# A mixture-of-experts pass that norms and stores its own tokens: gather, sum, norm and scatter moved from the kernel's end into each pass

## The chip, the cores and the metric

The kernel runs on one core of a Trainium2 chip. Its time is the device time of one execution in microseconds. The core has a matrix engine (TensorE, PE in the profile, with PEld for its weight loads), a vector engine (VectorE, DVE), a scalar engine (ScalarE, ACT), GpSimd (POOL), and SyncE (SP), which here only issues DMAs. Each engine runs its own instruction list in order and waits on semaphores for the others.

## The reference

One transformer layer on 512 tokens of width 1024, all in float32. First `proj = x @ w_in`, and three branches from it (an RWKV-7 scan over 8 heads, a gated spatial unit, a causal depthwise convolution), merged by sigmoid gates, then `x1 = layer_norm(ALPHA * x + merged @ w_out)`. What the change touches is the second half:

```
scores = sigmoid(x1 @ router_w)                    # 32 experts in 4 groups of 8
group  = the group whose two best scores sum highest
expert = the two best experts of that group, gate = their scores, normalised
moe    = sum over the two: gate * ((silu(x1 @ w_gate[e]) * (x1 @ w_up[e])) @ w_down[e])
out    = layer_norm(ALPHA * x1 + moe) * ln2_g + ln2_b
```

A token's two experts lie in one group; call the one with the lower index its lower expert, the other its upper expert.

## The kernel before

The stages follow each other on PE: projections and branches (to 469 us), the merge and `w_out` (to 585 us), the router and the tables of passes (to about 617 us), then the passes of the experts, and the last norm.

A pass (line 1456, `one_pass` of PE) takes up to 64 tokens of one expert. An expert with more than 64 tokens has more passes; here there are 33 for 32 experts, and the sixth expert has two. A token's row of 1024 values is laid over two partitions as two halves of 512, so 64 tokens fill 128 partitions (slots 0 to 63 hold the first halves, 64 to 127 the second). The order of a pass:

- POOL gathers the tokens' rows of `x1` from DRAM into `xe` by an indirect DMA (`gather`, L531), one pass ahead. An index out of bounds moves nothing, so empty slots cost no bytes.
- PE transposes `xe` (L1453) for the next pass; DVE copies it out as `xeT` (L1117).
- PE makes gate and up products (L1464): k = 0 to 7, two column halves, 16 products into each half of bank 0.
- ACT takes the silu (L718), DVE multiplies (L1110), PE transposes `h_e` (L1473), DVE copies (L1113), PE makes the down products (L1484) into bank 1.
- ACT scales the result by the gate into `y_e` (L722), and POOL scatters it to `y_dram` (L545), where a token has one row for its lower and one for its upper expert.

The weights of an expert are 6 chunks of 1 MB. Four sets of chunks are in SBUF. PE raises `s_used` as it is done with a chunk, and SP, which waits for that, issues the load of the same chunk for the expert four further on (`reload`, L450). SP's and POOL's DMAs go through different queues.

After the last passes SP loads `x1` back, the gains of the last norm (L457, L458), the lower rows (L463, as soon as all experts that can be lower are stored) and, after the last scatter, the upper rows in four parts (L467). DVE adds, takes mean and variance over 1024 values and norms each of the four parts of 128 tokens (L1131 to L1147), ACT takes the roots (L740), and SP stores each part (L470). Nothing is planned by a cost model: each engine's list is written out by hand, and semaphores alone set the order.

## Time and profile before

| | us |
|---|---|
| median of 3 runs | 1125.63 (1125.48 to 1126.07) |
| the profiled execution's own time | 1125.88 |
| its span, first to last instruction | 1124.2 |
| PE busy in the span | 982.6 (87%) |
| DVE, ACT, POOL busy | 359.7, 166.8, 123.9 |
| HBM read and written | 256.97 MB, 12.85 MB |
| mean granted TensorE clock | 0.965 of full speed |

The profile is one execution. Busy time counts an engine's instructions without waits. The slices cut the span into 40 equal parts. The chain of waits follows back from the last instruction to what released each step; "SPq" in it is SP issuing DMAs, "DMA a<-b" is a transfer in flight. In a timeline, the bracket says how long the engine was idle before the instruction and what ended that. PEld loads the stationary operand and overlaps PE. A window's row gives each engine's busy time and instruction count, then the granted clock, the DMA engines' busy share and GB/s.

### The profile page before, as it was taken

Reading aid. Unit: us, or ns where it says so; the run is one execution under the profiler, and the core shown is the slowest. Engines: PE = TensorE matmul, PEld = TensorE weight load, DVE = VectorE, ACT = ScalarE, POOL = GpSimd, SP = SyncE. Lnnn points to the kernel's source line nnn. Section 1 sums busy time; section 2 is a strip of 40 time slices with the busy share of each in tenths; the row PEclk is TensorE's granted clock in tenths of the full one; section 3 lists DMA queues with packets and bytes.
Section 4 is the critical chain, followed back from the end, with each engine's and each line's share of the span. In section 5 each row is a group of like instructions: output and inputs, shape, how many; then the busy total and the mean of one; then the engine's idle time right before and its main releaser. Section 6 shows DMA issues by size and latency. Waiting matters only on the chain.

```text
span 1124.2 us, 15343 instructions
## 1 busy us (share of the span) xinstructions
PE 982.6 (87%) x5932; PEld 457.0 (41%) x5933; DVE 359.7 (32%) x674; ACT 166.8 (15%) x304; POOL 123.9 (11%) x192
## 2 busy tenths in 40 slices
PE   7999999999999999999993688888888888887840
PEld 3644475466456457444453233333333333322210
DVE  0695643553463373422445000110000000000018
ACT  1123322312222222200001000000010000000010
POOL 1000010010010010033000111111111111111100
PEclk9999999999999999999995799999999999999985
DMA  8232201211220210573537799999999999999982
GB/s 254 61 92 58 74 22 38 76 39 39 56 58 21 66 48 10 213 295 151 219 115 322 270 420 419 396 419 421 419 419 418 419 421 419 420 420 421 420 316 117
DMA packets 90430, 261.35 MB, mean 232 GB/s; under 512 B 11192, under 2 KB 56248, under 8 KB 65552
## 3 DMA queue, kind: packets, MB, share of 16 engines
q1 hardware_dynamic: 83936, 249.46, 57.4%
q0 software_dynamic: 5648, 9.07, 2.2%
q10 hardware_dynamic: 800, 2.15, 0.5%
q8 instruction: 36, 0.59, 0.2%
q14 instruction: 10, 0.08, 0.0%
HBM read 256.97 MB, written 12.85 MB: 240 GB/s over the span
## 4 chain that ended last, share of the span: by engine, by line
PE 63%; SPq 14%; DVE 10%; DMA 8%; issue 4%; ACT 2%; DVEq 0%; ACTq 0%; POOLq 0%; PEldq 0%
SPq L450 13%; PE proj L1219 11%; PE bank L1464 10%; PE proj L1178 10%; PE bank L1484 6%; PE proj L1399 5%; PE bank L1309 5%; PE bank L1387 5%; DMA xT_sb<-w_gu 3%; DMA arena<-w_gu 2%; DMA gates<-y_rows 2%; PE proj L1186 1%; PE proj L1197 1%; DVE arena L867 1%; DVE arena L1117 1%
## 5 line engine op out<-in xcount | busy, mean ns | idle before, releaser
L1219 PE MATMUL proj<-xT_sb,ring 128*128 128x512 f32 x384 | 182.1, 607 | 0.0
L1110 DVE TENSOR_TENSOR const<-pass_sb,bank 128x256 f32<-128x256 f32 x33 | 13.9, 422 | 408.4 <-ACT pass_sb L718 408.4
L1464 PE MATMUL bank<-arena 128*64 128x512 f32 x544 | 122.2, 596 | 16.2 <-PE bank L1484 11.3
L1178 PE MATMUL proj<-xT_sb,ring 128*128 128x512 f32 (+1 forms) x272 | 119.1, 594 | 0.0
L1219 PEld LDWEIGHTS proj<-xT_sb,ring 128*128 128x128 f32 x384 | 68.2, 189 | 68.3 <-issue 64.8
L1464 PEld LDWEIGHTS bank<-arena 128*64 128x64 f32 x544 | 43.0, 137 | 95.2 <-issue 82.7
L1178 PEld LDWEIGHTS proj<-xT_sb,ring 128*128 128x128 f32 (+1 forms) x272 | 50.8, 188 | 64.6 <-issue 64.5
L1464 PE MATMUL bank<-gates,arena 128*64 128x512 f32 x256 | 59.7, 617 | 8.2 <-PE bank L1484 4.7
L1309 PEld LDWEIGHTS bank<-arena 64*64 64x64 f32 x1536 | 52.8, 134 | 18.2 <-ACT arena L676 9.1
L1309 PE MATMUL bank<-arena 64*64 64x64 f32 (+1 forms) x1536 | 56.5, 228 | 0.0
L1387 PE MATMUL bank<-branches,arena 128*128 128x512 f32 x128 | 55.4, 593 | 0.9 <-DVE branches L961 0.9
L1484 PE MATMUL bank<-arena,const 128*64 128x512 f32 x208 | 48.4, 600 | 8.8 <-DVE const L1113 8.8
L1399 PE MATMUL proj<-arena 128*128 128x512 f32 x128 | 55.4, 592 | 0.0
L545 POOL DMA_INDIRECT y_rows<-const,raw x33 | 33.7, 1020 | 147.7 <-ACT const L722 147.7
L718 ACT ACTIVATE pass_sb<-bank 128x256 f32<-128x256 f32 x33 | 12.7, 384 | 249.2 <-PE bank L1464 249.2
L722 ACT ACTIVATE const<-bank,raw 128x512 f32<-128x512 f32 x33 | 22.7, 687 | 178.7 <-PE bank L1484 178.7
L774 DVE SCALAR_TENSOR_TENSOR arena<-arena,par_sb 128x512 f32<-128x512 f32 x60 | 39.8, 742 | 0.0
L531 POOL DMA_INDIRECT pass_sb<-x_rows,raw x34 | 35.8, 1052 | 26.9 <-POOL raw L528 26.1
L528 POOL COPY raw<-raw 128x1 int32 (+1 forms) x34 | 6.2, 183 | 295.0 <-PE bank L1453 206.9
L1464 PEld LDWEIGHTS bank<-gates,arena 128*64 128x64 f32 x256 | 18.4, 141 | 49.1 <-issue 43.2
L1387 PEld LDWEIGHTS bank<-branches,arena 128*128 128x128 f32 x128 | 24.2, 190 | 31.9 <-issue 30.1
L676 ACT ACTIVATE arena<-bank 128x256 f32<-128x256 f32 (+1 forms) x64 | 27.5, 436 | 64.6 <-PE bank L1309 59.6
(259 smaller groups left out, 1011.1 us busy)
## 6 DMA issues: line engine op xcount, KB each, us to landing
arena<-w_gu SPq DMA_DIRECT2D x64, 1024.0 KB, 24.6
gates<-w_gu SPq DMA_DIRECT2D x32, 1024.0 KB, 21.9
arena<-w_down SPq DMA_DIRECT2D x24, 1024.0 KB, 24.7
ring<-w_in SPq DMA_DIRECT2D x42, 512.0 KB, 3.9
gates<-w_down SPq DMA_DIRECT2D x16, 1024.0 KB, 23.5
branches<-w_down SPq DMA_DIRECT2D x16, 1024.0 KB, 25.9
xT_sb<-w_gu SPq DMA_DIRECT2D x16, 1024.0 KB, 26.4
ring<-w_gu SPq DMA_DIRECT2D x16, 1024.0 KB, 25.8
```

What stands on the lines that cost most here:

```text
L450: sp.dma_start(w_chunk[b][c], src.rearrange("a p n -> (a p) n")).then_inc(s_w[b][c], 16)
L531: pool.indirect_dma_start(xe, None, x1_dram, bass.IndirectOffsetOnAxis(ap=idx_now[:, 0:1], axis=0), bounds_check=last_half_row, oob_is_err ...
L545: pool.indirect_dma_start(y_dram, bass.IndirectOffsetOnAxis(ap=row_now[:, 0:1], axis=0), y_e, None, bounds_check=last_row, oob_is_err=Fals ...
L676: ins = act.activation(d, bank[:, 3 * g + b, 0:TT * n].rearrange("p (j n) -> p j n", j=TT), ACT.Copy)
L774: ins = dve.scalar_tensor_tensor(conv_acc[:, i, :], src, w, conv_acc[:, i, :], MUL, ADD)
L1178: ins = pe.matmul(proj[0:w, b, :], ring[:, slot, k, 0:w], xT_sb[:, k, :], start=(k == 0), stop=(k == KT - 1))
L1219: ins = pe.matmul(proj[:, gate_at["bank"], :], ring[:, gate_at["slot"], k, :], xT_sb[:, k, :], start=(k == 0), stop=(k == KT - 1))
L1309: ins = pe.matmul(bank[t, 3 * g + b, j * n:j * n + n], lhsT[t, j, :], rhs[t, j, :], start=True, stop=True)
L1387: ins = pe.matmul(bank[:, 3 * (m % 2) + n, :], wo_sb[:, k0 + k, m * P:(m + 1) * P], src[:, k, :], start=(k == 0), stop=(k == nk - 1))
L1399: ins = pe.matmul(proj[:, n % 2, :], merged[:, k, c * P:(c + 1) * P], wout_sb[:, k, T * i:T * i + T], start=(k == 0), stop=(k == KT - 1))
L1464: ins = pe.matmul(bank[SLOTS * h:SLOTS * h + SLOTS, 0, :], xeT[:, k % 4, SLOTS * (k // 4):SLOTS * (k // 4) + SLOTS], gu[k // 2][:, k % 2, ...
L1484: ins = pe.matmul(bank[SLOTS * h:SLOTS * h + SLOTS, 1, :], hT[:, f % 2, SLOTS * (f // 2):SLOTS * (f // 2) + SLOTS], wd[f // 2][:, f % 2, h ...
```

## The change

In each pass, the tokens for which its expert is the upper one are finished. Their lower rows are already in `y_dram`, because experts run in order of index.

- `y_dram` now has one row per token, for the lower expert alone. It is zeroed early by eight DMAs on POOL. POOL scatters `y_e` there with `low_tab`, whose index is out of bounds for upper tokens (`scatter_lower`).
- POOL gathers, with `up_tab`, the lower rows of a pass's upper tokens into `y_low` (`lower_rows`), after the last pass's lower scatter has landed.
- ACT copies the token rows times ALPHA from `xe` into PSUM, by turns bank 5 and bank 4 (`keep_rows`); the next token gather waits for that too.
- DVE (`finish`) adds `y_low`, then `y_e`, into `x2`, and takes mean and variance over each half row (512 values). The two halves of a token sit on different partitions: PE adds them by a product with `ident_twice` (`pair_stats`), at k = 4 of the next pass's gate and up products. Then DVE and ACT make the deviation, and DVE scales twice, with the gains now in the two banks of `proj`.
- POOL scatters `x2` to the output with `up_tab` (`scatter_out`).
- `h_silu` and `h_e` now share one place, and `hT` too; the extra pass's ACT work waits for one bank more.
- SP's reloads at the end, the last norm and the four stores are gone. SP loads the gains (4 DMAs of 64 partitions x 2 KB) when the tables are ready.

POOL's order in a pass p is now: the token gather of p+2, the lower scatter of p, the output scatter of p, the lower rows of p+1. DVE's is: products of p, then `finish` of p.

```diff
+        x_now, ln2_g, ln2_b = (bank[:, 5, :], bank[:, 4, :]), proj[:, 0, :], proj[:, 1, :]
+        pair = bank[:, 3, FE // 2:FE // 2 + 2]
...
+            sp.wait_ge(s_more, 1)
+            for i, dst in ((0, y_e), (1, x2)):
+                for h in range(2):
+                    at = 2 * SGU + 2 * D + D * i + T * h
+                    sp.dma_start(dst[SLOTS * h:SLOTS * h + SLOTS, :],
+                                 rows[:, at:at + T].partition_broadcast(SLOTS).rearrange("p a d -> p (a d)")).then_inc(s_lnback, 16)
...
-            sp.wait_ge(s_used, (N_EXP - 3) * NCH + 1)
...
-            sp.dma_start(y_lower, y_rows[0]).then_inc(s_lower, 16)
-            more = sp.value_load(more_i[0:1, 0:1], min_val=0, max_val=MORE)
-            sp.wait_ge(s_yst, more * 16 + 16 * N_EXP)
-            for c in range(TT):
-                sp.dma_start(y_upper[:, c, :], y_rows[1, :, c, :]).then_inc(s_upper[c], 16)
-            for c in range(TT):
-                sp.wait_ge(s_x2[c], 1)
-                sp.dma_start(out[c * P:(c + 1) * P, :], x1_back[:, c, :]).then_inc(s_st, 16)
-            sp.wait_ge(s_st, 16 * TT)
...
+            for n in range(T // SLOTS):
+                pool.dma_start(y_dram.rearrange("(n s h) d -> n s (h d)", s=SLOTS, h=2)[n], zeros).then_inc(s_y0, 16)
...
+            def lower_rows(p, first=False):
+                pool.tensor_copy(up_now[:, 0:1], up_tab[:, bass.ds(p, 1)]).then_inc(s_up, 1)
+                pool.wait_ge(s_up, p + 1)
+                if not first:
+                    pool.wait_ge(s_yst, p * 16)
+                pool.sem_inc(s_begun, 1)
+                pool.indirect_dma_start(y_low, None, y_dram, bass.IndirectOffsetOnAxis(ap=up_now[:, 0:1], axis=0),
+                                        bounds_check=last_half_row, oob_is_err=False).then_inc(s_ylow, 16)
+            def scatter_lower(p):
+                pool.tensor_copy(low_now[:, 0:1], low_tab[:, bass.ds(p, 1)]).then_inc(s_low, 1)
+                pool.wait_ge(s_low, p + 1)
                 pool.wait_ge(s_ye, p + 2)
                 pool.sem_inc(s_begun, 1)
-                pool.indirect_dma_start(y_dram, bass.IndirectOffsetOnAxis(ap=row_now[:, 0:1], axis=0), y_e, None,
-                                        bounds_check=last_row, oob_is_err=False).then_inc(s_yst, 16)
-            def one_pass(p):
-                next_tokens(p + 2)
-                pool.wait_ge(s_yst, p * 16 + 16)
-                scatter(p + 1)
+                pool.indirect_dma_start(y_dram, bass.IndirectOffsetOnAxis(ap=low_now[:, 0:1], axis=0), y_e, None,
+                                        bounds_check=last_half_row, oob_is_err=False).then_inc(s_yst, 16)
+            def scatter_out(p, first=False):
+                if not first:
+                    pool.wait_ge(s_ost, p * 16)
+                pool.tensor_copy(out_now[:, 0:1], up_tab[:, bass.ds(p, 1)]).then_inc(s_outidx, 1)
+                pool.wait_ge(s_outidx, p + 1)
+                pool.wait_ge(s_x2, p + 1)
+                pool.sem_inc(s_begun, 1)
+                pool.indirect_dma_start(out_dram, bass.IndirectOffsetOnAxis(ap=out_now[:, 0:1], axis=0), x2, None,
+                                        bounds_check=last_half_row, oob_is_err=False).then_inc(s_ost, 16)
+            def one_pass(p, first=False):
+                next_tokens(p + 1)
+                scatter_lower(p)
+                scatter_out(p, first)
+                pool.wait_ge(s_ylow, p * 16 + 16)
+                lower_rows(p + 1)
...
+            scatter_out(more + (N_EXP - 1))
...
+            def keep_rows(p, n):
+                act.wait_ge(s_xe, p * 16 + 16)
+                act.activation(x_now[n], xe, ACT.Copy, scale=ALPHA).then_inc(s_xnow, 1)
+            def one_pass(p, n, first=False):
                 act.activation(warm[:, 1:2], warm[:, 0:1], ACT.Silu)
                 act.wait_ge(s_hp, p + 1)
-                act.activation(h_silu, bank[:, 0, 0:FE // 2], ACT.Silu).then_inc(s_silu, 1)
+                act.activation(h_e, bank[:, 0, 0:FE // 2], ACT.Silu).then_inc(s_silu, 1)
+                act.wait_ge(s_base, p + (2 if n is None else 1))
+                keep_rows(p + 1, 0 if n is None else 1 - n)
+                if first:
+                    act.wait_ge(s_gains, 1)
+                else:
+                    act.wait_ge(s_yst, p * 16)
+                    act.wait_ge(s_sum, p)
                 act.wait_ge(s_yp, p + 2)
-            def store_ready(p):
                 act.activation(y_e, bank[:, 1, :], ACT.Copy, scale=gate_tab[:, bass.ds(p, 1)]).then_inc(s_ye, 1)
-            def later_pass(p):
-                one_pass(p + 1)
-                act.wait_ge(s_yst, p * 16 + 16)
-                store_ready(p + 1)
-            one_pass(0)
-            store_ready(0)
-            with act.Fori(0, N_EXP - 1) as i:
-                later_pass(i)
+                act.activation(warm[:, 2:3], warm[:, 0:1], ACT.Sqrt)
+                act.wait_ge(s_dev, p + 1)
+                act.activation(half_rs[:, 2:3], pair[:, 1:2], ACT.Sqrt, bias=half_rs[:, 1:2], scale=0.5).then_inc(s_root, 1)
...
+                dve.wait_ge(s_xnow, p + 1)
+                dve.wait_ge(s_ylow, p * 16 + 16)
+                if not first:
+                    dve.wait_ge(s_ost, p * 16)
+                dve.tensor_tensor(x2, x_now[n], y_low, ADD).then_inc(s_base, 1)
+                dve.wait_ge(s_base, p + 2)
+                dve.wait_ge(s_ye, p + 2)
+                dve.tensor_tensor(x2, x2, y_e, ADD).then_inc(s_sum, 1)
+                dve.wait_ge(s_sum, p + 1)
+                dve.bn_stats(ln_stat[:, 0, 0:6], x2).then_inc(s_norm2, 1)
+                dve.wait_ge(s_norm2, p * 4 + 1)
+                dve.memset(half_rs[:, 3:4], 0.0)
+                dve.bn_aggr(half_mv, ln_stat[:, 0, 0:6]).then_inc(s_stat, 1)
+                dve.wait_ge(s_pair, p + 2)
+                dve.tensor_scalar(mean, pair[:, 0:1], 0.5, None, MUL)
+                dve.scalar_tensor_tensor(dev_in, pair[:, 0:1], -0.5, half_mv[:, 0:1], MUL, ADD).then_inc(s_norm2, 1)
+                dve.wait_ge(s_norm2, p * 4 + 2)
+                dve.tensor_scalar(dev_in, dev_in, dev_in, LN_EPS, MUL, ADD).then_inc(s_dev, 1)
+                dve.scalar_tensor_tensor(x2, x2, mean, ln2_g, SUB, MUL).then_inc(s_norm2, 1)
+                dve.wait_ge(s_root, p + 1)
+                dve.reciprocal(root, root).then_inc(s_norm2, 1)
+                dve.wait_ge(s_norm2, p * 4 + 4)
+                dve.scalar_tensor_tensor(x2, x2, root, ln2_b, MUL, ADD).then_inc(s_x2, 1)
...
-            def variance(c):
-                dve.wait_ge(s_upper[c], 16)
-                then(dve.tensor_tensor(x1_back[:, c, :], x1_back[:, c, :], y_upper[:, c, :], ADD))
-                for i in range(2):
-                    ins = dve.bn_stats(ln_stat[:, c, 6 * i:6 * i + 6], x1_back[:, c, T * i:T * i + T])
-                then(ins)
-                then(dve.bn_aggr(ln_mv[:, c, :], ln_stat[:, c, :]))
-                dve.tensor_scalar(ln_rs[:, c:c + 1], ln_mv[:, c, 1:2], LN_EPS, None, ADD).then_inc(s_lnvar2, 1)
-            def normed(c):
-                dve.wait_ge(s_lnroot2, c + 1)
-                then(dve.reciprocal(ln_rs[:, c:c + 1], ln_rs[:, c:c + 1]))
-                then(dve.scalar_tensor_tensor(x1_back[:, c, :], x1_back[:, c, :], ln_mv[:, c, 0:1], ln2_rows[:, 0, :], SUB, MUL))
-                dve.scalar_tensor_tensor(x1_back[:, c, :], x1_back[:, c, :], ln_rs[:, c:c + 1], ln2_rows[:, 1, :], MUL, ADD).then_inc(s_x2[c], 1)
...
+            def pair_stats(p):
+                pe.wait_ge(s_stat, p + 1)
+                for h in range(2):
+                    ins = pe.matmul(pair[SLOTS * h:SLOTS * h + SLOTS, :], C("ident_twice"), ln_mv[:, 0, :], start=True, stop=True)
+                ins.then_inc(s_pair, 1)
             def one_pass(p, b, loads, last):
                 pe.wait_ge(s_xeT, p + 1)
                 gu = [v.rearrange("p (k h n) -> p k h n", k=2, h=2) for v in w_chunk[b][0:4]]
                 for k in range(KT):
+                    if k == 4:
+                        pair_stats(p)
...
+            pair_stats(more + N_EXP)
```

## Rows read from the trace of the kernel before

**Rows 1.** The page's slices: what the DMA engines moved, 28.1 us each

```profile
GB/s 254 61 92 58 74 22 38 76 39 39 56 58 21 66 48 10 213 295 151 219 115 322 270 420 419 396 419 421 419 419 418 419 421 419 420 420 421 420 316 117
```

**Rows 2.** Chain of waits, by time: start us, us, engine and line

```profile
642.88 7.10 PE bank L1464 x32
...
709.31 6.89 PE bank L1464 x32
...
1032.83 27.55 DMA arena<-w_gu
...
1076.68 17.19 DMA gates<-y_rows
```

**Rows 3.** Timeline of one pass: start us, us, what, idle before and its releaser

```profile
802.80 7.09 PE L1464 MATMUL bank<-gates,arena 128*64 128x512 f32 x32 [0.67 <-PE bank L1484]
...
811.62 1.05 POOL L531 DMA_INDIRECT pass_sb<-x_rows,raw  x1 [0.79 <-POOL raw L528]
...
811.85 3.65 PE L1484 MATMUL bank<-gates,const 128*64 128x512 f32 x16 [0.52 <-DVE const L1113]
...
812.67 0.20 POOL L541 COPY raw<-raw 128x1 int32 x1
...
815.73 0.69 ACT L722 ACTIVATE const<-bank,raw 128x512 f32<-128x512 f32 x1 [5.42 <-PE bank L1484]
...
816.18 7.09 PE L1464 MATMUL bank<-arena 128*64 128x512 f32 x32 [0.68 <-PE bank L1484]
...
817.23 1.01 POOL L545 DMA_INDIRECT y_rows<-const,raw  x1 [4.37 <-ACT const L722]
```

**Rows 4.** Timeline of the end, all engines

```profile
1076.06 1.94 PE L1464 MATMUL bank<-xT_sb,arena 128*64 128x512 f32 x8 [1.18 <-DMA xT_sb<-w_gu]
...
1079.96 3.65 PE L1484 MATMUL bank<-branches,const 128*64 128x512 f32 x16 [0.52 <-DVE const L1113]
...
1091.27 1.98 SPq L467 DMA_DIRECT2D arena<-y_rows  x4
...
1119.83 1.28 DVE L1147 SCALAR_TENSOR_TENSOR gates<-gates,arena 128x1024 f32<-128x1024 f32 x1
```

**Rows 5.** Groups by shape, VectorE, and one of ScalarE: busy us, mean ns of one, idle before

```profile
L774 DVE SCALAR_TENSOR_TENSOR arena<-arena,par_sb 128x512 f32<-128x512 f32 x60 | 39.8, 742 | 0.0
...
L942 DVE TENSOR_TENSOR arena<-bank,arena 128x512 f32<-128x512 f32 x16 | 11.1, 692 | 21.2 <-PE bank L1350 20.9
...
L1138 DVE BATCH_NORM_STATS2 arena<-gates 128x6 f32<-128x512 f32 x8 | 5.1, 686 | 0.1
...
L1141 DVE TENSOR_SCALAR arena<-arena 128x1 f32<-128x1 f32 x4 | 0.6, 154 | 0.1
...
L740 ACT ACT_TABLE_LOAD x1 | 1.3, 1283 | 0.0
```

**Rows 6.** Landings: gathers L531, scatters L545, gathers at 626.4 and 1064.1 (us last)

```profile
DMA to landing us min/median/max: 2.9/6.7/7.3
...
DMA to landing us min/median/max: 5.9/6.6/7.5
...
pass_sb<-x_rows,raw POOLq DMA_INDIRECT x1, 2.9
...
pass_sb<-x_rows,raw POOLq DMA_INDIRECT x1, 6.3
```

**Rows 7.** Window 702:716; SP's request behind it; POOL's queue in 820:1050

```profile
702.00:716.00 14.00, 13.07 (x62) 4.34 (x58) 1.38 (x3) 1.16 (x3) 2.44 (x4) 1.00 0.96 369
...
711.21 6.51 SPq L450 DMA_DIRECT2D arena<-w_gu  x4
...
q0 software_dynamic: 2640, 4.00, 4.7%
```

**Rows 8.** Window 20:30 (PEclk, DMA share, GB/s last), and POOL's next work

```profile
20.00:30.00 10.00, 10.00 (x24) 4.29 (x23) 0.00 (x0) 3.05 (x4) 0.63 (x1) 1.00 0.54 144
...
106.44 2.25 POOL L492 MEMSET arena<- 64x512 f32 x4 [83.57 <-DVE branches L840]
```

More of the change, by code:

```diff
@@ L736, in _ @@
                 with act.Fori(0, more) as i:
[L737 to L740 removed]
+                    one_pass(i + N_EXP, None)
         @block.vector
@@ L1119, in _ @@
             turned(0)
-            with dve.Fori(0, N_EXP) as i:
-                one_pass(i)
-            dve.wait_ge(s_more, 1)
+            dve.sem_inc(s_base, 1)
+            dve.sem_inc(s_stat, 1)
+            products(0)
+            dve.wait_ge(s_lnback, 64)
+            dve.tensor_copy(ln2_g, y_e)
+            dve.tensor_copy(ln2_b, x2).then_inc(s_gains, 1)
+            dve.wait_ge(s_gains, 1)
+            finish(0, 0, first=True)
+            products(1)
+            finish(1, 1)
+            with dve.Fori(1, N_EXP // 2) as i:
+                for n in range(2):
+                    p = dve.snap(i * 2 + n, min_val=2, max_val=N_EXP - 1)
+                    products(p)
+                    finish(p, n)
             more = dve.value_load(more_i[0:1, 0:1], min_val=0, max_val=MORE)
```

124 lines of the change are left out of this document (62 added, 62 removed).

## The prediction

> **What bounds the kernel now.** I read the page's slices first, then the chain of waits, one pass as a timeline, the landings, and the end as a timeline. From about 645 us the DMA engines run at 415 to 420 GB/s, nearly to the end [rows 1], so the expert weights look like the bound. The chain says less: the first passes follow each other on PE, and only the end hangs on weights in flight [rows 2]. A pass whose weights are there takes 802.80 to 816.18 = 13.38 us of PE, a serial chain: gate and up products 7.09, transposes and copies, down products to 815.50, 0.68 to the next [rows 3]. The second of the 33 passes starts at 642.88 [rows 2]; at 13.38 each they would end the down products at 642.88 + 32 x 13.38 - 0.68 = 1070.4. They end at 1079.96 + 3.65 = 1083.6 [rows 4]. So the weight stream costs only 13 us more than PE alone: passes may become 0.4 us longer on average before they pass the stream. That is the number to hold on to. Behind the passes lie 1124.2 - 1083.6 = 40.6 us: last scatter, reload of rows, four norms, stores [rows 4].
>
> **The change, part by part.** I call T the moment in a pass at which PE reaches k = 4, the middle of gate and up, where it now makes the pair statistics. It lies 3.4 us behind the pass's start (half of 7.09, less the 0.1 by which the last end lags), and the down products end 815.50 - 802.80 - 3.4 = 9.3 us behind T [rows 3].
>
> *The tail.* All 40.6 us go. In their place, from the end of the down products: 0.23 + 0.69 for y_e on ACT [rows 3]; sum 0.69, bn_stats 0.69, aggregate about 0.16, hops of 0.04 each and a short memset [rows 5]: 2.6 us. Then the pair product on PE, 0.45 (estimate: two weight loads of 0.14 to 0.2 with two-column products, below the two full transposes' own 0.44), and on DVE 0.15 + 0.07 + 0.15 for the small steps, 0.75 for the first scaling (begun beside them), 0.15, 0.75 and hops, 2.0 us, with ACT's root 0.2 beside the first scaling. That makes 5.1. POOL starts an indirect DMA 0.81 us behind what it waits for (816.42 to 817.23) [rows 3]. The landing then lies between 2.9 (unloaded) and 6.7 (beside the stream) [rows 6]; with all weights in I take 4, as it is a write. Tail: 10 us, bounds 9 to 14.
>
> *The loop that the change makes.* This sets my forecast. Norms were off every pass's path. Now PE at T of pass p+1 waits for the statistics of pass p. These need the lower rows of p, and POOL fetches them only behind the scatter of the output rows of p-1, which waits for the x2 of p-1, and that needs the pair product at T of pass p. From T to the next T, once PE waits:
> pair product 0.45; DVE to x2 2.0; POOL's start 0.81; its DMA instruction 1.02; index copy 0.20 and 0.79 to the next DMA [rows 3]; landing 6.7 [rows 6]; base sum 0.69, sum 0.69, bn_stats 0.69, memset and aggregate 0.2, hops 0.2, together 2.45 [rows 5]. Sum 14.4 us. The direct pass is 13.4 and some 0.15 for the pair product. So every pass from the third on takes 14.4, a stall of about 0.9.
> Two terms need bounds. The landing: the gather of 626.4, in a quiet stretch, landed after 2.9; that of 1064.11, one pass beyond the last and so without a row to fetch, still took 6.3 beside the stream, and the medians are 6.6 and 6.7, the longest 7.5 [rows 6]. The stream, not the rows, makes it long, so few lower rows don't help: 6.3 to 7.5, and I take 6.7. The y_low gather goes out 2.0 us behind another transfer of the same queue; before, two of that queue lay 5.6 apart (811.62, 817.23), so no row shows that neighbour: 0 to 1.7 (worked out in the second rival), I take 0, as transfers of either kind have the same median. Loop: 14.0 to 16.1.
> A second loop runs over two passes: y_e of p at T + 0.45 + 9.3 + 0.92 = 10.7; lower scatter landed 7.4 later; gather issued 0.8 and landed 6.7 later; sums and statistics 2.45: 28.1 for two passes, 14.05 each. It is just behind the first and holds the pass near 14.05 even if the first is quicker.
>
> The Trainium skill weighs against my landing. Its page "DMA: Bandwidth & Descriptors", section "Anatomy of one DMA — SWDGE (gpsimd) path", fits a POOL-issued DMA as 2.0 us and its bytes over 436 KB per us. The 2.9 of the quiet stretch is near that; the 6.7 of the loaded stretch is not, and there the row decides. By the page's figure the loop would be some 10 us and never bind; that is the first rival.
>
> *When the pair point lies.* y_e of pass 0 ended at about 642.9, its statistics by 644.6, T of pass 1 is 642.88 + 3.4 = 646.3: no wait. The two gains' rows (0.5 MB, asked for when the tables are ready, near 617) are needed by y_e of pass 0 at 642: 0, or once what they come late. From there T(32) = 646.3 + 31 x 14.4 = 1092.7, less about 1 us, since the last fetch before it starts as the stream runs out. Down products end 1091.7 + 0.45 + 9.3 = 1101.4.
>
> *The stream.* SP's requests ran dry once: the sixth and seventh pass belong to one expert, SP's next request waits for a freed chunk until 711.21, and the rate falls to 369 GB/s in 702 to 716 [rows 7]. So what is late at 711 is late for the stream. T(6) comes at 646.3 + 5 x 14.4 = 718.3, its pass starts at 714.9 against 709.31 [rows 2]: 5.6 later. To it come more bytes: two indirect DMAs per pass become four, while 1024 rows of 4 KB in and 1024 out become 1024 in, 512 out, 512 in, 512 out; half again 512 x 4 KB = 2.1 MB, over 26 of 33 passes at 420 GB/s 4 us, and a little for more descriptors: 4.4. (Beside the stream the POOL queue takes 4.7% of the engines [rows 7].) PE waited last for a chunk at 1076.06 [rows 4]; this becomes 1086, and PE now needs it at T(32) + 1.7 = 1093.4. The stream is no longer the bound, and what comes later in it costs nothing; without loop stalls it would be.
>
> *Small edits.* Eight zeroing DMAs of 256 KB go out on POOL near 23 us, when the DMA engines are half idle [rows 8], and POOL has nothing else until 106.44: 0, at most 2. The index tables lie under the first gather's flight: 0. ACT loads two tables more per pass, 1.28 each [rows 5]. The Sqrt load lies between y_e and the root, both sides with 3 us to spare; the Silu load starts at T + 1.2 and ends at T + 2.5, its product needs it at T + 4: nothing, and if that cover went, up to 1.3 a pass. The moved token gather is issued at T + 7.5 and lands at T + 14; PE transposes at T + 18: 0.
>
> **Sum.** 1101.4 + 10 = 1111.4 span, plus 1125.88 - 1124.2 = 1.7 around it: 1113.1. The median of the runs is 0.25 under the profiled one: 1113. That is 12.7 us faster, where the tail alone would give 30.
>
> **Rivals.**
> *A, the loop does not bind* (landings near 2.9, or overlap that I miss). The stream sets the end: 1.5 late at 711, 4.4 of bytes, down products at 1083.6 + 5.9 = 1089.5, tail 10, 1.7 around: 1101. For it: the quiet landing; against it: the medians of all the others. Chance 0.15.
> *B, slower: the fetch of lower rows queues behind the output scatter of the same queue.* Place: the landing term. If its data part, 6.6 - 2.9 = 3.7, starts only when the scatter has landed, it ends 0.81 + 6.7 + 3.7 = 11.2 behind x2 instead of 9.5, the pass is 16.1, and the time 1113 + 31 x 1.7 = 1166. It decides from 12.6 / 31 = 0.41 us more per pass; a third of it gives 1131. For it: one queue, two DMAs 2 us apart; against it: the row-less gather took as long as full ones, so the time is mostly latency, which overlaps. Any other 0.41 us in the loop (register arithmetic before the many counted waits of DVE and POOL) does the same. Chance 0.25, most of it between 1128 and 1145.
> *C, near balance:* loop at 14.75 to 14.9, the tail's gain given back: 1125. Chance 0.08.
> *D, the tail does not shrink* because the last pass's lower rows come late: their gather goes out at T(32) + 5.3, 4.5 before the down products end, and would have to take 30 us. 0.01, counted with B.
> My forecast, loop of 14.05 to 14.7: 1102 to 1123, chance 0.52.
>
> **Range and chances.** 1101 to 1134 holds the floor by the stream, the whole forecast, and B up to 15.1 us a pass; 0.15 lies above it and 0.05 below. A difference under 0.2%, 2.3 us, can't be told from none. Faster (forecast and A): 0.67. Same: 0.08. Slower: 0.25.
>
> **What would show it.** Passes of 14.4 us between starts from the third on, with PE idle at k = 4 behind DVE's aggregate and not behind weights; y_low's gather landing after 6.3 to 7.5; POOL's output scatter 0.8 behind x2; PE's waits for weight chunks gone from the last third; 10 us from the last down product to the end. Passes of 13.5 and waits on weights show A; landings of y_low over 7.5 show B. The prediction is wrong if the loop's sum is: 0.1 us in it is 3.1 us in the time.

## The result, and the profile of the changed kernel

The changed kernel takes **1116.35 us** (median of 4 runs, 1114.33 to 1117.91), the kernel before 1125.56 (4 runs, 1125.40 to 1126.07): ratio 0.9916, 95% interval 0.9903 to 0.9928. It is 9.2 us faster; 12.6 were forecast, and 1116.35 lies 3.3 us above the 1113.0 of the prediction, inside its range. The profiled execution has a span of 1112.6 us.

Where the time went, from the two traces: the down products end at 1098.06 + 3.65 = 1101.7 instead of 1083.6 [rows 4], 18.1 later; behind them lie 10.9 us instead of 40.6, 29.7 less. Together 11.6 less, which is 1124.2 - 1112.6.

The timeline of one pass of the changed kernel, from one pair product to the next (start us, us, what, idle time before it and its releaser); it answers to [rows 3]:

```profile
804.97 0.28 PE L1507 MATMUL bank<-arena,const 128*64 128x2 f32 x4 [0.84 <-DVE arena L1166]
...
806.54 0.75 DVE L1176 SCALAR_TENSOR_TENSOR raw<-raw,half_rs,proj 128x512 f32<-128x512 f32 x1
...
808.12 1.01 POOL L564 DMA_INDIRECT out<-raw  x1 [5.45 <-DVE raw L1176]
...
809.13 0.19 POOL L539 COPY raw<-raw 128x1 int32 x1
...
810.17 1.07 POOL L544 DMA_INDIRECT const<-y_rows,raw  x1 [0.84 <-POOL raw L539]
...
816.95 0.69 DVE L1158 TENSOR_TENSOR raw<-bank,const 128x512 f32<-128x512 f32 x1 [6.29 <-DMA const<-y_rows,raw]
...
817.67 0.69 DVE L1161 TENSOR_TENSOR raw<-raw,const 128x512 f32<-128x512 f32 x1
...
818.40 0.69 DVE L1163 BATCH_NORM_STATS2 arena<-raw 128x6 f32<-128x512 f32 x1
...
819.37 0.28 PE L1507 MATMUL bank<-arena,const 128*64 128x2 f32 x4 [0.69 <-DVE arena L1166]
```

The reader is to see a closed loop: PE waited for DVE's aggregate (L1166), x2 is ready at 806.54 + 0.75 = 807.29, POOL sends the output scatter, copies the index and sends the fetch of lower rows, DVE waits for that fetch, and 14.40 us after the first pair product stands the next, again behind L1166.

What PE waited for between 640 and 1110 us (line, releaser: us in total, times, longest):

```profile
PE bank L1507 <- DVE arena L1166: 23.5, 31, 3.3
PE bank L1520 <- PE bank L1540: 21.3, 31, 0.8
PE bank L1540 <- DVE pass_sb L1147: 15.0, 29, 0.5
```

The first is the new wait. Its last one, 2.71 us, stands before the pair product at 1104.42, behind all passes; the 30 in the passes share 20.8 us, 0.7 each, and the longest has 3.3. No weight chunk is among PE's releasers: the wait at 1076.06 of before [rows 4] has no counterpart. The chain of waits (start us, us, what) runs through one fetch per pass; these are the first four, two of the middle and the last:

```profile
652.17 7.43 DMA const<-y_rows,raw
667.30 7.42 DMA const<-y_rows,raw
682.36 7.22 DMA const<-y_rows,raw
697.22 6.55 DMA const<-y_rows,raw
...
881.57 6.35 DMA const<-y_rows,raw
895.57 6.48 DMA const<-y_rows,raw
...
1083.24 6.64 DMA const<-y_rows,raw
```

The end as a timeline, in the places of [rows 4]:

```profile
1097.54 1.07 POOL L544 DMA_INDIRECT const<-y_rows,raw  x1 [0.85 <-POOL raw L539]
...
1098.06 3.65 PE L1540 MATMUL bank<-branches,pass_sb 128*64 128x512 f32 x16 [0.52 <-DVE pass_sb L1147]
...
1100.40 0.69 DVE L1158 TENSOR_TENSOR raw<-bank,const 128x512 f32<-128x512 f32 x1 [2.39 <-DMA const<-y_rows,raw]
...
1107.76 1.01 POOL L564 DMA_INDIRECT out<-raw  x1 [8.95 <-DVE raw L1176]
```

The last fetch runs when the weights are in, and the base sum starts 2.86 us behind it instead of 6.4 to 6.9. The last output scatter takes the 4.8 us from 1107.76 to the end.

### The profile page after: what moved, and what is told of

The parts are those of the page before. It is cut to its first block, busy times and chain, and to the rows that moved or that the text cites. A ratio compares the mean times of both kernels' runs of the same rounds, so it can differ in the third digit from the quotient of the medians.

```text
span 1112.6 us, 16547 instructions
## 1 busy us (share of the span) xinstructions
PE 989.5 (89%) x6068; PEld 456.1 (41%) x6069; DVE 472.8 (42%) x1006; ACT 283.9 (26%) x464; POOL 208.9 (19%) x331
## 3 DMA queue, kind: packets, MB, share of 16 engines
q0 software_dynamic: 11104, 13.29, 3.5%
## 4 chain that ended last, share of the span: by engine, by line
PE 51%; DMA 18%; DVE 16%; issue 8%; POOL 3%; ACT 1%; POOLq 1%; SPq 0%; DVEq 0%; ACTq 0%
DMA const<-y_rows,raw 18%; PE proj L1267 11%; PE proj L1226 11%; PE proj L1447 5%; PE bank L1357 5%; PE bank L1435 5%; POOL out L564 3%; DVE raw L1176 2%; PE bank L1520 2%; DVE raw L1161 2%; DVE raw L1158 2%; PE proj L1234 1%; PE proj L1245 1%; DVE arena L897 1%; DVE raw L1172 1%
## 5 line engine op out<-in xcount | busy, mean ns | idle before, releaser
L1158 DVE TENSOR_TENSOR raw<-bank,const 128x512 f32<-128x512 f32 x33 | 22.8, 692 | 196.6 <-DMA const<-y_rows,raw 196.5
L1520 PEld LDWEIGHTS bank<-arena 128*64 128x64 f32 x544 | 39.7, 137 | 80.5 <-issue 80.5
L564 POOL DMA_INDIRECT out<-raw x33 | 33.3, 1008 | 178.3 <-DVE raw L1176 165.1
L1540 PE MATMUL bank<-arena,pass_sb 128*64 128x512 f32 x208 | 48.4, 600 | 8.8 <-DVE pass_sb L1147 7.8
L1144 DVE TENSOR_TENSOR pass_sb<-pass_sb,bank 128x256 f32<-128x256 f32 x33 | 13.9, 421 | 74.0 <-ACT pass_sb L745 68.1
L528 POOL DMA_INDIRECT pass_sb<-x_rows,raw x34 | 35.7, 1050 | 28.3 <-POOL raw L525 27.2
```

Of the source, the lines that this page charges most:

```text
L528: pool.indirect_dma_start(xe, None, x1_dram, bass.IndirectOffsetOnAxis(ap=idx_now[:, 0:1], axis=0), bounds_check=last_half_row, oob_is_err ...
L564: pool.indirect_dma_start(out_dram, bass.IndirectOffsetOnAxis(ap=out_now[:, 0:1], axis=0), x2, None, bounds_check=last_half_row, oob_is_er ...
L1158: dve.tensor_tensor(x2, x_now[n], y_low, ADD).then_inc(s_base, 1)
L1520: ins = pe.matmul(bank[SLOTS * h:SLOTS * h + SLOTS, 0, :], xeT[:, k % 4, SLOTS * (k // 4):SLOTS * (k // 4) + SLOTS], gu[k // 2][:, k % 2, ...
L1540: ins = pe.matmul(bank[SLOTS * h:SLOTS * h + SLOTS, 1, :], hT[:, f % 2, SLOTS * (f // 2):SLOTS * (f // 2) + SLOTS], wd[f // 2][:, f % 2, h ...
```

## Experiments

Each diff is against the changed kernel unless it says otherwise. "Pass" is the time between two pair products. Theory: the loop of the norms sets the pass. Rivals: a queueing of the two POOL DMAs, the weight stream, the rows that are fetched. The diffs are shortened: "..." stands for code left out, and helper definitions are not shown.

### The pair product one step later (k = 5)

```diff
-                    if k == 4:
+                    if k == 5:
                         pair_stats(p)
```

> The changed kernel with the pair statistics at k = 5 instead of k = 4, 0.86 us later in PE's pass. Loop theory: the period is set by the closed chain statistics -> pair product -> x2 -> output scatter -> fetch of the lower rows -> sums -> statistics, whatever the place at which PE waits; so passes stay at 14.4 us, and the time at 1116 (1114 to 1118). Rival (PE simply arrives 0.9 us too early after the down products): moving the point by 0.86 us takes the stall away, passes of 13.55 us, the weight stream becomes the bound, 1095 to 1103.

Measured: 1115.6 us (1114.02 to 1116.13), ratio 0.9906 (0.9888 to 0.9924), passes of mostly 14.0 to 14.3 as before (the first ones and the 29th are longer here too). Giving PE 0.9 us more before it needs the statistics buys nothing, as in a closed loop: the point moves with the loop. The rival (the point is only too early for PE) falls.

### The pair product at the pass's start (k = 0)

```diff
-                    if k == 4:
+                    if k == 0:
                         pair_stats(p)
```

> The changed kernel with the pair statistics at k = 0, 3.43 us earlier in PE's pass. The first loop has no term of PE's products and would leave the time at 1116. The second loop (y_e of p, its lower scatter's landing, the fetch of lower rows for p+1, sums, statistics, PE's point in p+2) grows from 27.6 to 31.0 us for two passes and becomes the longer: 15.5 us a pass, 31 x 1.1 = 34 us more, 1150. Rival (only the first loop exists): 1116. Rival (PE arrives too early): 31 x 3.43 = 106 us more, 1222.

Measured: 1202.35 us (1200.92 to 1207.14), ratio 1.0695 (1.0666 to 1.0723); passes of 17.07. The expectation was missed by 52 us. I had named a second loop and not the plainest one. Timeline of this kernel:

```profile
864.04 0.69 ACT L754 ACTIVATE const<-bank,raw 128x512 f32<-128x512 f32 x1 [4.83 <-PE bank L1540]
864.83 0.69 DVE L1161 TENSOR_TENSOR raw<-raw,const 128x512 f32<-128x512 f32 x1 [1.00 <-ACT const L754]
...
865.56 0.69 DVE L1163 BATCH_NORM_STATS2 arena<-raw 128x6 f32<-128x512 f32 x1
866.29 0.18 DVE L1166 BATCH_NORM_AGGREGATE arena<-arena 128x2 f32<-128x6 f32 x1
...
866.62 0.38 PE L1507 MATMUL bank<-arena,const 128*64 128x2 f32 x4 [2.72 <-DVE arena L1166]
```

The down products of the pass must be scaled, summed and measured before PE may begin the next pass: PE stands idle for 2.72 us in every pass, however quick the fetch. With 2.72 in place of the 0.67 between passes [rows 3] the 13.38 become 15.43, and the pair product adds 0.21 (gate and up start at 866.83). The rest, 1.4, is the clock. Windows of this kernel (us, busy times of PE, PEld, DVE, ACT, POOL, then granted clock, DMA share, GB/s), and the gate and up products' group in 840 to 1000 (busy us, mean ns) of this kernel and then of the changed one:

```profile
850.00:866.00 16.00, 12.97 (x54) 4.27 (x52) 5.08 (x12) 4.57 (x7) 4.13 (x7) 0.92 0.97 373
866.00:884.00 18.00, 13.74 (x64) 5.04 (x66) 5.97 (x17) 5.02 (x10) 5.65 (x10) 0.89 0.99 392
```

```profile
L1520 PE MATMUL bank<-arena 128*64 128x512 f32 x128 | 34.1, 692 | 0.0
```

```profile
L1520 PE MATMUL bank<-arena 128*64 128x512 f32 x160 | 36.4, 596 | 3.4 <-PE bank L1540 3.4
```

With 2.72 us of idleness ahead of each pass the granted clock is 0.92 and 0.89 as a mean, so a part of each stretch runs at 1.2 instead of 2.4 GHz, and a product takes 692 instead of 596 ns. The gate and up products of a pass, which nothing cuts in two here, take 8.53 us, where the kernel before had 7.09 [rows 3]: 1.44 more. The changed kernel's wait of 0.7 us at k = 4 leaves the clock at 1.00.

### The fetch ahead of the output scatter

```diff
                 scatter_lower(p)
-                scatter_out(p, first)
                 pool.wait_ge(s_ylow, p * 16 + 16)
+                lower_index(p + 1)
+                pool.wait_ge(s_base, p + 2)
                 lower_rows(p + 1)
+                scatter_out(p, first)
```

(`lower_index` is the index copy of `lower_rows`, made a step of its own.)

> The changed kernel with POOL's order turned: the lower rows of p+1 are fetched before the output scatter of p, behind the lower scatter's landing and the sum that has read y_low. Loop theory: the fetch no longer waits for x2 and lands 0.7 to 1 us sooner, but the output scatter now starts some 1.9 to 3.5 us later, and the next base sum waits for it because there is one x2: from x2's end or the fetch's issue, copy and start 1.0, landing 6.6, sums 2.45. Passes of about 15.1 us, 1138 (1130 to 1145). Rival (only the fetch's issue counts): passes of 13.8, 1101.

Measured: 1147.43 us (1141.23 to 1150.57), ratio 1.0192 (1.0147 to 1.0237): 2.4 us above the 1130 to 1145 that were expected. Passes go up and down between 13.5 and 16.8 (12.6 and 18.3 once each), 15.3 on average over the 31 from 647.69 to 1122.58. Timeline of this kernel:

```profile
851.64 1.05 POOL L545 DMA_INDIRECT const<-y_rows,raw  x1 [6.12 <-DMA y_rows<-const,raw]
...
853.76 1.02 POOL L565 DMA_INDIRECT out<-raw  x1 [0.87 <-POOL raw L561]
...
860.57 0.69 DVE L1162 TENSOR_TENSOR raw<-bank,const 128x512 f32<-128x512 f32 x1 [8.13 <-DMA out<-raw]
```

DVE's base sum waits for the landing of the output scatter, since both use the one x2, and that scatter now goes out second. The wait has changed its owner and grown. A part of the slowness is again the clock: with waits of mostly 2 to 3.5 us at every other pair product the granted clock in 820 to 940 us is 0.96, where the changed kernel has 1.00.

### The same with two x2 tiles by turns

Against the kernel just above (not shown: the index tables move to a tile of their own, and POOL's loop holds two passes instead of one):

```diff
-            def scatter_out(p, first=False):
+            def scatter_out(p, n, first=False):
...
-                IndirectOffsetOnAxis(ap=out_now[:, 0:1], axis=0), x2, None,
+                IndirectOffsetOnAxis(ap=out_now[:, 0:1], axis=0), x2s[n], None,
...
-                    dve.wait_ge(s_ost, p * 16)
+                    dve.wait_ge(s_ost, p * 16 if extra else p * 16 - 16)
```

> As rows_first, but with two x2 by turns (the index tables move to a tile of their own), so that no sum waits for the output scatter of the pass before. Loop theory: the first loop is cut, the second remains with 27.6 us for two passes = 13.8 us a pass, against a bare pass of 13.6; 0.57 x 31 = 18 us less than 1116 by PE, but the weight stream then ends near the passes: 1099 to 1105. Rival (landings grow as transfers of POOL's queue overlap, or the norm's instructions themselves lengthen the pass): 1116 or more.

Measured: 1109.62 us (1108.55 to 1111.68), ratio 0.9862 (0.9842 to 0.9882). The passes from 759 to 1007 came out at 13.5 to 14.0 (mean 13.8), as expected; the first ones were longer, up to 15.0, and behind 1007 they are 14.3 to 16.7. With the first loop cut, the prediction's second loop is left: in all 18 passes from 760 to 1000 the fetch waits for the landing of the lower scatter, as here, though PE waits for the statistics in few of them:

```profile
880.53 1.03 POOL L556 DMA_INDIRECT y_rows<-const,tables  x1 [0.99 <-ACT const L766]
...
888.26 1.05 POOL L546 DMA_INDIRECT const<-y_rows,tables  x1 [6.10 <-DMA y_rows<-const,tables]
```

This kernel also answers the rival of a queueing. The last output scatter lies some 11 us ahead of the fetch here, and still the fetch's median landing (from issue to the base sum) is 6.64 us, against 6.60 in the changed kernel, where it goes out 2.05 behind the scatter.

The expected time was 4 to 5 us too optimistic, and the reason is this line, with the weights as releaser:

```profile
1088.70 1.94 PE L1533 MATMUL bank<-xT_sb,arena 128*64 128x512 f32 x8 [0.57 <-DMA xT_sb<-w_gu]
```

Its counterpart of before stands at 1076.06 [rows 4]: 12.6 later. As soon as the loop is shorter, the weight stream is the bound again, and it is later than I worked out.

### The index copied ahead of the wait for x2

```diff
                 scatter_lower(p)
-                scatter_out(p, first)
                 pool.wait_ge(s_ylow, p * 16 + 16)
+                lower_index(p + 1)
+                scatter_out(p, first)
                 lower_rows(p + 1)
```

> The changed kernel with the index copy for the next fetch of lower rows made before POOL waits for x2, not after the output scatter. In the loop, 1.03 us lie between the end of the output scatter's instruction and the fetch (copy 0.19, start 0.84). Loop theory: at least the copy's 0.2 goes, at most all 1.03, down to the second loop's 13.8 us: passes of 13.8 to 14.2. By PE alone that is 6 to 18 us less than 1116, but the weight stream ends the passes of two_x2 at 1109.6 already, so 1108 to 1112. Rival (the fetch's issue is not on the chain that sets the pass): 1116.

Measured: 1109.31 us (1108.04 to 1110.53), ratio 0.986 (0.9844 to 0.9877), as expected. Timeline of this kernel:

```profile
832.12 1.00 POOL L565 DMA_INDIRECT out<-raw  x1 [4.11 <-DVE raw L1179]
833.48 1.05 POOL L545 DMA_INDIRECT const<-y_rows,raw  x1 [0.36 <-issue]
```

From scatter to fetch 1.36 us, where the changed kernel has 810.17 - 808.12 = 2.05. The pass falls by some 0.5, from 14.3 to 13.8, by one copy of 0.2 us put where POOL waits anyway. It only moves one step of POOL, needs no second tile, and beats both the changed kernel and the one before. This kernel too ends on the stream: PE waits for `xT_sb<-w_gu` at 1088.37.

### No lower rows fetched

```diff
-                pool.tensor_copy(up_now[:, 0:1], up_tab[:, bass.ds(p, 1)]).then_inc(s_up, 1)
+                pool.tensor_copy(up_now[:, 0:1], idx_tab[:, PASSES - 1:PASSES]).then_inc(s_up, 1)
```

> The changed kernel with an index out of bounds for every slot of the fetch of lower rows: the DMA is issued and moves no row, so the lower experts' part is left out of the output. Theory (a transfer of POOL's queue lands late because the stream keeps the DMA engines busy, not because of its rows): landing still 6.3 to 6.7, passes 14.2 to 14.4, 1113 to 1117. Rival (its rows make it long): landing near 3, the first loop at 10.6, passes of 13.6, the stream as the bound, 1104 to 1110.

Measured: 1110.95 us (1110.29 to 1111.6), ratio 0.9873 (0.9853 to 0.9893). This kernel leaves the lower experts' part out of its output. With not one row to fetch, issue and landing are:

```profile
864.58 1.07 POOL L545 DMA_INDIRECT const<-y_rows,raw  x1 [0.84 <-issue]
871.01 0.69 DVE L1159 TENSOR_TENSOR raw<-bank,const 128x512 f32<-128x512 f32 x1 [5.96 <-DMA const<-y_rows,raw]
```

6.43 us, which is also the median of this kernel, against a median of 6.60 in the changed kernel. The rows cost 0.2 us of a landing; the pass falls by as much, from 14.25 to 14.07. What does not fall is the number of packets: POOL's queue has 11104 in either kernel, with 11.20 MB instead of 13.29. The expectation had the landing right and the time 2 us too high, since it gave the rows nothing.

### An eighth of the weights, in the changed kernel and in the one before

```diff
+THIN = CHUNK // 8
...
-                    src = w_gu[bass.ds(e, 1), :, n:n + CHUNK] if n < GU else w_down[bass.ds(e, 1), :, n - GU:n - GU + CHUNK]
-                    sp.dma_start(w_chunk[b][c], src.rearrange("a p n -> (a p) n")).then_inc(s_w[b][c], 16)
+                    src = w_gu[bass.ds(e, 1), :, n:n + THIN] if n < GU else w_down[bass.ds(e, 1), :, n - GU:n - GU + THIN]
+                    sp.dma_start(w_chunk[b][c][:, 0:THIN], src.rearrange("a p n -> (a p) n")).then_inc(s_w[b][c], 16)
```

> The changed kernel with each reload of weights fetching one eighth of its columns (the rest of a chunk keeps the earlier expert's weights, so the output of experts from the fifth on is another). DMA engines mostly idle in the passes. Theory: the fetch lands after about 2.9, the first loop shrinks to 10.6 us, PE never waits: passes of 13.38 + 0.15 = 13.55, down products' end at 647 + 31 x 13.55 + 9.4 = 1076.5, tail 10.9, time 1089. Rival (the norm's instructions and waits in the pass lengthen it by themselves): passes stay at 14.4, 1116.

> The kernel before with the same thin reloads. Passes of 13.38 to the end, down products' end near 1070.4, then its tail of 40.6 us less what the busy DMA engines cost it (the reload of x1 and of the lower rows no longer queues behind weights: 4 to 8 us): 1105 to 1110. With thin_after near 1089 the difference is what the change is worth where nothing loaded the DMA engines: 31 us off the tail, 0.15 x 33 = 5 and 1 us at the start given back, -16 to -22. Rival (the tail was long for other reasons than its own work): more.

Measured: 1086.91 us (1086.67 to 1087.14), ratio 0.9659, for the changed kernel, and 1106.17 (1105.84 to 1106.49), ratio 0.983, for the one before. The second is as expected, the first 2 us under the expected 1089, as its passes are 13.49 and not 13.55. Both leave the experts from the fifth on with mostly older weights. Timeline and window (180 us, DMA share 0.27, 79 GB/s) of the changed kernel with thin weights:

```profile
827.52 1.07 POOL L545 DMA_INDIRECT const<-y_rows,raw  x1 [0.84 <-POOL raw L540]
...
830.35 0.69 DVE L1159 TENSOR_TENSOR raw<-bank,const 128x512 f32<-128x512 f32 x1 [2.35 <-DMA const<-y_rows,raw]
```

```profile
820.00:1000.00 180.00, 159.07 (x780) 58.47 (x778) 74.71 (x191) 64.33 (x108) 65.18 (x106) 1.00 0.27 79
```

The same fetch lands after 2.83 us, passes take 13.49, and PE no longer waits for the statistics in any pass. So of the 6.4 to 7.4 us of a landing nearly 4 are the price of the weight stream beside the fetch. The kernel before has passes of 13.37 with thin weights (1029.80, 1043.17, 1056.54), so the pair product costs PE 0.12 us a pass. The change alone, without the stream, is worth 19.3 us; with it 9.2.

### Two x2 tiles in the old order, and the two ideas together with k = 5

Two last kernels with more runs each. The first is the changed kernel with the x2 tiles of above and POOL's order as it was:

```diff
                 scatter_lower(p)
-                scatter_out(p, first)
+                scatter_out(p, n, first)
                 pool.wait_ge(s_ylow, p * 16 + 16)
+                lower_index(p + 1)
                 lower_rows(p + 1)
```

> The changed kernel's own order on POOL (output scatter, then the fetch of lower rows), but with two x2 tiles by turns and the index copy ahead of the output scatter. My theory: the second x2 tile buys nothing by itself, since x2 of a pass is overwritten only a pass later and the scatter that reads it has landed by then; what counts is the time from x2 to the fetch, and that is the one of index_early (1.36 us). So passes of 13.6 to 14.0 and 1108 to 1112, the same as index_early. Rival: the tile is what gave two_x2 its short passes, because DVE then no longer waits for the output scatter's landing; then this kernel has passes of 13.4 to 13.5, and it comes in under 1107 or ends on the weight stream.

Measured: 1118.24 us (1116.62 to 1119.63), ratio 0.993 (0.9916 to 0.9943), passes of 14.3. Missed, and for a plain reason: as the diff shows, the index copy stands behind the output scatter and not ahead of it, as the expectation says. The timeline has it there:

```profile
838.01 1.00 POOL L568 DMA_INDIRECT out<-raw,tables  x1 [5.18 <-DVE raw L1188]
839.02 0.19 POOL L539 COPY tables<-tables 128x1 int32 x1
...
840.05 1.06 POOL L546 DMA_INDIRECT const<-y_rows,tables  x1 [0.84 <-ACT bank L751]
```

2.04 us from scatter to fetch, and the pass of the changed kernel; its time is 1.9 us longer, with overlapping intervals. What it tells is narrower and still useful: the second tile alone buys nothing, and what separates this kernel from the one with the early copy, apart from the tile, are the 0.7 us between scatter and fetch. The rival (the tile made the passes short) falls in this order of POOL; with the fetch first it was the tile that took the passes from 15.3 to 13.8.

The second is the kernel with the fetch first and two x2 tiles, and against it:

```diff
-                    if k == 4:
+                    if k == 5:
                         pair_stats(p)
```

> two_x2 with the pair statistics one step of k later (k = 5). two_x2 ended on the weight stream: PE waited for chunks at 1088.7. My theory: the stream sets its end, so 0.9 us more room in every pass changes nothing there: 1108 to 1111, passes of 13.5 to 13.7 before 1000 and waits on weight chunks at the end. Rival: the passes of 13.8 set it (a loop of the norms again); then the pass falls to 13.5 and the time by some 5 us or more, to 1100 to 1105.

Measured: 1107.17 us (1104.67 to 1108.31), ratio 0.9835 (0.9821 to 0.9848), the fastest kernel here by a little; its interval overlaps those of the early copy and of two x2 tiles, and the time is 0.8 under the 1108 to 1111 expected. The theory that the later point changes nothing was half right. Passes of 13.5 to 13.9 until 987, on average 13.6 where k = 4 has 13.8, so waits for the statistics did still lengthen those; the 13.5 and the 5 us of the rival did not come, since the passes behind are 15.0 to 16.6. What PE waited for in this kernel:

```profile
PE bank L1533 <- DMA arena<-w_gu: 8.0, 11, 1.4
PE bank L1520 <- DVE arena L1179: 4.1, 5, 2.7
PE bank L1533 <- DMA xT_sb<-w_gu: 2.8, 4, 0.9
PE bank L1533 <- DMA ring<-w_gu: 2.0, 3, 0.8
```

Of the 30 waits for the statistics in the passes four are left, 1.4 us in all (the fifth here, of 2.7, is the one behind the passes), and the weights have taken their place. Here the stream's price can be read with hardly any delay of the request: SP's request behind the dry stretch goes out at 711.83, almost as before at 711.21 [rows 7], and yet PE's last wait for a chunk is this one:

```profile
1084.39 1.94 PE L1533 MATMUL bank<-xT_sb,arena 128*64 128x512 f32 x8 [0.46 <-DMA xT_sb<-w_gu]
```

1084.39 - 1076.06 = 8.3 us later, of which 0.6 are the request: 7.7 us for the change's own DMAs. The same reading gives 8.3 in the kernel with the early copy (request at 715.24, last wait at 1088.37) and 9.2 in the one with two x2 tiles (714.60, 1088.70), so 7.7 is the low end.

### The late output scatter of pass 28

In the changed kernel the 29th interval between pair products is 17.03 us; in six of its variants above it is 16.5 to 18.3, and in a seventh, with two x2 tiles and k = 5, it is 15.8 among others as long, with POOL late at the same pass. With k = 0, where passes have room, it is 17.3 among 17.07. Where the fetch goes out first, it is the fetch that is late (with two x2 tiles at 1028.95, 16.6 behind the one before). The kernel before shows no such step. POOL's timeline there, in the changed kernel; x2 was ready at 1034.88:

```profile
1030.13 0.19 POOL L560 COPY raw<-raw 128x1 int32 x1
1038.38 1.01 POOL L564 DMA_INDIRECT out<-raw  x1 [8.06 <-issue]
1039.40 0.19 POOL L539 COPY raw<-raw 128x1 int32 x1
```

3.5 us from x2 to the scatter, where 0.8 is the rule. Two kernels asked whether the number of POOL's DMAs, or of the row pieces in them, places it; both cut the eight zeroing DMAs into 24 (shortened; each kernel has one of the last two lines):

```diff
-                pool.dma_start(... [n], zeros).then_inc(s_y0, 16)
+                for lo, hi in zip(cuts, cuts[1:]):
+                    pool.dma_start(y_n[lo:hi], zeros[lo:hi]).then_inc(s_y0, 16)         # by rows
+                    pool.dma_start(y_n[:, lo:hi], zeros[:, lo:hi]).then_inc(s_y0, 16)   # by columns
```

> The changed kernel, its eight zeroing DMAs cut into 24 by rows (two of the eight in nine pieces each; same bytes). It asks about one thing: in every kernel with the new passes POOL starts one DMA some 2.5 us late, the output scatter of pass 28 (in the changed kernel at 1038.38 instead of about 1035.7; x2 was ready at 1034.88), also with one weight byte in eight, at 1017.03. Before it the POOL queue has sent 131 DMAs: 14 direct ones, 31 gathers of tokens, 29 fetches and 29 scatters of lower rows, 28 output scatters. My theory: the delay belongs to the number of DMAs sent by POOL. Then 16 more, at four per pass, move it 4 passes earlier: the long pass of about 17.0 us comes at the 25th instead of the 29th interval between pair points, near 978 to 993, and the 29th is 14.3. Rivals: it belongs to the rows or descriptors moved, which hardly change here (moved by under one pass), or to the pass itself (its data, or the code of the loop): then it stays in pass 28. The time stays at 1116 in each case, plus or minus 2.

> The changed kernel, its eight zeroing DMAs cut into 24 by columns (each in three pieces of 256, 256 and 512 columns, 64 rows each; same bytes, three times the row pieces). If the number of POOL's DMAs places the delayed output scatter, it moves 4 passes earlier as with the cut by rows (long interval of about 17.0 at the 25th). If the number of row pieces does, 16 more of 64 rows move it by about 4 passes if an indirect DMA counts 64, or 2 if it counts 128, while the cut by rows leaves it. If it belongs to the pass, it stays at the 29th. Time 1116, plus or minus 2.

Measured: 1115.28 and 1115.95 us, ratios 0.9913 (0.9884 to 0.9941) and 0.9919 (0.989 to 0.9947). The delay did not move, first in the cut by rows, then by columns:

```profile
1038.38 1.01 POOL L567 DMA_INDIRECT out<-raw  x1 [7.82 <-issue]
```

```profile
1037.87 1.01 POOL L567 DMA_INDIRECT out<-raw  x1 [7.72 <-issue]
```

Intervals 25 to 28 are 14.0 to 14.5 in both, the 29th 16.92 and 16.85. My theory of the count falls; the delay belongs to pass 28. A much smaller one did move with the count: in the changed kernel the 27th output scatter is 0.2 us late too (1.04 us behind x2 instead of 0.83), and in the two cut kernels it is not, while the fetch behind the 24th is (2.20 and 2.25 behind its scatter instead of 2.05). With thin weights it is there too (POOL's scatters at 1001.08, 1017.03 and 1027.84, where 13.5 apart is the rule), so it isn't the traffic. What in that pass delays POOL, its data or a value that POOL waits for, stays open. It costs 2.8 us once in the changed kernel.

## Why the prediction was right, step by step

- **What bounds.** The step that set the forecast, that PE at k = 4 waits for a loop through POOL's two DMAs, is what the trace shows. The loop's terms, predicted and then measured in the pass from 804.97: pair product and DVE to x2 2.45 and 2.32; POOL's start 0.81 and 0.83; its DMA instruction 1.02 and 1.01; copy and next start 0.99 and 1.04; landing 6.7 and 6.78; sums and statistics 2.45 and 2.42. Sum 14.4 and 14.40. Over 31 passes, from 646.98 to 1092.33, the mean is 14.37.
- **The second loop.** Predicted at 14.05 a pass, just behind the first. Where the first is cut (two x2 tiles, fetch first) the pass is 13.8, and moving the pair point by one k takes it to 13.6. So the loop is there, close behind PE's own 13.5, and 0.25 or more shorter than predicted.
- **The landing.** That a transfer beside the stream of 416 GB/s takes 6 to 7 us whatever it carries was borne out three ways: 6.4 us without a row, 2.83 without the stream, 2.86 for the last fetch. The Trainium skill's page "DMA: Bandwidth & Descriptors", section "Anatomy of one DMA — SWDGE (gpsimd) path", with 2.0 us and the bytes over 436 KB per us, is near the unloaded ones and far from the loaded ones, as the prediction weighed it. "Few rows don't help" was right but for 0.2 us. The fetch 2 us behind another transfer of its queue: I took 0 of 0 to 1.7, and the medians bear that out, 6.60 in this place and 6.64 and 6.7 in the two kernels with two x2 tiles that send it first. Why the landings of the first three passes are 7.2 to 7.4 is not shown; in the two kernels with two x2 tiles that send the fetch first they are 6.9 to 8.0, so the output scatter ahead is not the reason.
- **The first passes.** Four of them took 59.24 us in sum, 2.2 more than four of the later ones at 14.25, and the fetches' landings of 7.43, 7.42, 7.22 and 6.55, together 2.2 above four times 6.6, account for it. I had taken one median for all.
- **T(32) and the end.** Predicted 1091.7, measured 1092.33; down products' end 1101.4 and 1101.7. This agreement has a cancellation in it. Against 14.4 each, the first four passes were 1.6 longer and the one with the late scatter 2.6; the interval from 706.22 to 718.97, where the stream is dry, the fetch lands after 5.06 and none stands in the chain, was 1.65 shorter (PE alone needs less there, the second pass of one expert: 12.62 with thin weights, where the others take 13.49), and the 25 others, with a mean of 14.25, 3.7 in sum. That leaves 1.05 less, where the forecast had taken off 1 for another reason. The same short pass is why the 1070.4 that the prediction worked out for PE alone is a little late: with thin weights the kernel before ends its down products at 1069.2.
- **The tail.** 10 predicted, 10.9 measured. The term that was small is the last scatter, 4 taken and 4.8 measured.
- **What was mis-sized: the stream.** "To it come more bytes: ... 4.4" was 7.7 at the least (8.3 and 9.2 in two other kernels). The slices and windows show the rate of the steady stretch at 416 GB/s (760 to 1000 us) instead of 419 to 421 [rows 1]; over the 380 us from 711 to 1090 that 1% is 3.6 us on top of the 4 us of bytes, which makes 7.6. I had put the descriptors at 0.4. That it is the number of transfers and not their bytes shows in the kernel that fetches no row: in 820 to 1050 us its POOL queue moves 3.71 MB, less than the 4.00 of before, in 5120 packets, and the rate is 416 all the same. In the changed kernel SP's request also went out later, at 717.51 against 711.21 [rows 7], 6.3 and not 5.6. None of it showed in the time, as the prediction said for a stream that isn't the bound, but it decides how much a shorter loop can give: 1107 to 1109, and not the 1101 of rival A.
- **The rivals.** A (no loop) happens with thin weights. B needed landings over 7.5; the longest was 7.43. C did not occur. D neither: the tail shrank as worked out.
- **The 3.3 us of miss** are spread: the profiled span is 1.2 above the predicted one (0.3 in the passes, 0.9 in the tail), and the median of the runs lies 2.0 above the profiled execution's 1114.33, where before it lay 0.3 below. In these four runs each the new kernel scatters more (3.6 us against 0.7; but seven runs of the kernel before, measured beside the k = 5 kernel, went from 1124.23 to 1127.84), and a median can't be had from one profile of before.
- **A dependency that I didn't list**: y_e of a pass to the statistics to the next pair product. At k = 4 it has slack; the experiment at k = 0 shows that it would have cost 2.7 us a pass and the clock.

## What to carry to other kernels

When work is moved into a loop, add up the closed loop through every engine and queue it crosses and compare it with the pass it rides on: here 14.4 against 13.5, and the passes gave back 18 of the 30 us that the removed tail brought (the stream alone would have taken some 8 of them, by the kernel with two x2 tiles and k = 5). A transfer issued in such a loop counts with its landing beside the traffic of that loop, not with its unloaded one, and everything that its engine does between the releasing event and its issue (here an index copy, 0.7 us with its start) should be done ahead of the wait. When the loop is cut, look for what stands right behind it: the stream had only a few us of room, and a second buffer for x2 on its own gave nothing.

## What the runs showed of the hardware that was not expected

- A POOL DMA that moves no row lands after 6.4 us beside a saturated weight stream and one with rows after 2.83 where the stream is thin: the load matters, the size hardly (0.2 us here).
- Two more small indirect DMAs per pass lower the rate of all DMAs together by 1%, 416 instead of 420 GB/s, and that without rows in the fetch as well. The POOL queue in 820 to 1050 us: 5169 packets and 5.9% of the engines, against 2640 and 4.7% [rows 7].
- PE waits of 2.7 us in each pass lower the granted clock to about 0.9 and lengthen the products from 596 to 692 ns; waits of 0.7 us, at k = 4, leave it at 1.00.
- POOL sends one DMA some 2.7 us late in pass 28 of every kernel with the new passes, whatever the load and with 16 more DMAs before it too. Its cause is open.
